# One-core transformer kernel: the first shift and scale made as columns by TensorE, S5's matrices scaled later, the experts' routing weights and masks reordered

## The reference, cut to what matters

```python
c_act = silu(c)
mod = c_act @ w_ada + b_ada                       # [1024] @ [1024, 6144]
sh1, sc1, gt1, sh2, sc2, gt2 = split(mod, 6)
a_in = rmsnorm(h, norm1_g) * (1 + sc1) + sh1
mix = concat(s5_mixer(...), gdn_mixer(...)) @ w_out   # both from a_in @ w_in
h = h + gt1 * mix
m_in = rmsnorm(h, norm2_g) * (1 + sc2) + sh2
moe = hier_moe(m_in, ...)   # 4 groups of 8 experts; per token one group and its top 2 experts
h = h + gt2 * moe
```

## Time and profile before

| | |
|---|---|
| median of 3 runs | 2877.12 us (2876.14 to 2879.36) |
| the profiled execution | 2873.54 us, its span 2871.7 us |
| mean granted clock of TensorE | 0.98 |
| busy: TensorE, its weight load, VectorE, ScalarE, GpSimd | 2752.7, 2308.8, 1597.9, 1233.0, 140.9 us |
| moved by DMA | 509.35 MB, mean 177 GB/s |

### The profile page before, as it was taken

One profiled execution on the slowest core, in us unless ns is written; L12 is line 12 of the kernel. 1 busy time (PEld: TensorE's weight loads), 2 busy tenths in 40 slices (PEclk: granted clock), 3 DMA queues, 4 the chain that ended last, 5 costly groups with the idle time before them and its releaser, 6 DMA issues. The chain is left out here.

```text
span 2871.7 us, 35302 instructions
## 1 busy us (share of the span) xinstructions
PE 2752.7 (96%) x14506; PEld 2308.8 (80%) x14506; DVE 1597.9 (56%) x1821; ACT 1233.0 (43%) x1588; POOL 140.9 (5%) x227
## 2 busy tenths in 40 slices
PE   7988979999999999999998999999999999999998
PEld 6977877888788887888887888888878888896887
DVE  5884467767644536445455645545454464544544
ACT  3202245656534445344344434434453443444443
POOL 4000000000000100001000000000000010010000
PEclk9998989999999999999999999999999999999999
DMA  7432056878655544656553755554435556452652
GB/s 249 156 108 88 30 200 229 310 279 297 220 181 176 167 138 136 207 189 213 193 166 107 240 182 176 191 187 153 144 118 183 195 178 206 155 169 90 225 176 88
DMA packets 349485, 509.35 MB, mean 177 GB/s; under 512 B 14880, under 2 KB 295488, under 8 KB 349328
## 3 DMA queue, kind: packets, MB, share of 16 engines
q1 hardware_dynamic: 342960, 484.17, 49.9%
q0 software_dynamic: 5792, 20.78, 2.1%
q10 hardware_dynamic: 576, 2.20, 0.2%
HBM read 506.04 MB, written 1.05 MB: 177 GB/s over the span
## 5 line engine op out<-in xcount | busy, mean ns | idle before, releaser
L393 DVE TENSOR_TENSOR raw_r<-raw,whi 128x2048 fp32r<-128x2048 f32 x185 | 421.9, 2290 | 170.3 <-ACT whi L385 169.3
L833 ACT ACTIVATE h_hi<-psum 128x256 fp32r<-128x256 f32 x216 | 82.8, 383 | 758.5 <-PE psum L772 684.2
L385 ACT ACTIVATE whi<-raw 128x2048 fp32r<-128x2048 f32 x185 | 351.1, 1909 | 12.4 <-DMA raw<-in_w_up 6.7
L888 DVE TENSOR_TENSOR h_lo<-psum,h_hi 128x256 fp32r<-128x256 f32 x216 | 91.5, 424 | 437.1 <-ACT h_hi L833 437.1
L407 PE MATMUL psum<-place_lo,act_hi 128*128 128x512 f32 (+1 forms) x840 | 318.6, 379 | 0.0
L406 PE MATMUL psum<-whi,act_hi 128*128 128x512 f32 (+1 forms) x872 | 308.2, 353 | 5.4 <-DVE act_lo L639 4.3
L408 PE MATMUL psum<-whi,act_lo 128*128 128x512 f32 (+1 forms) x872 | 302.1, 346 | 0.0
L393 DVE TENSOR_TENSOR place_lo<-arena,place_hi 128x2048 fp32r<-128x2048 f32 x107 | 244.2, 2289 | 91.8 <-ACT place_hi L385 91.8
L407 PE MATMUL psum<-raw_r,act_hi 128*128 128x512 f32 (+1 forms) x808 | 283.8, 351 | 0.0
L406 PE MATMUL psum<-place_hi,act_hi 128*128 128x512 f32 (+1 forms) x592 | 234.1, 395 | 0.0
L408 PE MATMUL psum<-place_hi,act_lo 128*128 128x512 f32 (+1 forms) x592 | 228.6, 386 | 0.0
(11 more groups left out here) (537 smaller groups left out, 5832.7 us busy)
## 6 DMA issues: line engine op xcount, KB each, us to landing
arena<-in_ff_w_in SPq DMA_DIRECT2D x182, 512.0 KB, 4.9
raw<-in_ff_w_in SPq DMA_DIRECT2D x126, 512.0 KB, 4.9
arena<-in_ff_w_out SPq DMA_DIRECT2D x88, 512.0 KB, 4.5
raw<-in_ff_w_out SPq DMA_DIRECT2D x68, 512.0 KB, 4.5
wlo_f<-in_ff_w_in SPq DMA_DIRECT2D x44, 512.0 KB, 4.9
raw<-in_w_ada SPq DMA_DIRECT2D x20, 1024.0 KB, 5.2
raw<-in_w_gate SPq DMA_DIRECT2D x35, 512.0 KB, 4.4
raw<-in_w_up SPq DMA_DIRECT2D x35, 512.0 KB, 5.4
```

What stands on the lines that cost most here:

```text
L385: act.activation(hi, loaded, ACT.Copy).then_inc(S("slab_hi"), 1)
L393: dve.tensor_tensor(lo, loaded, hi.bitcast(F32), ALU.subtract).then_inc(S("slab_lo"), 1)
L833: act.activation(pair_of(turned_h[0], g), gate_up(g)[:, 0:256], ACT.Copy).then_inc(S("pass_turned_hi"), 1)
L888: dve.tensor_tensor(pair_of(turned_h[1], g), gate_up(g)[:, 0:256], pair_of(turned_h[0], g).bitcast(F32), ALU.subtract)\
```

## The change

1. The eight slabs of sh1 and sc1: the slab's 128x128 blocks become the stationary operand and one column of c_act moves past, 16 matmuls per slab instead of 8. The result is a column, 128 values on 128 partitions, in banks 2 and 3. `mod_dve` reads it from there with b_ada (L1157). VectorE's work on `diag` is gone for these slabs, and with it TensorE's wait for it.
2. `s5_c_dve` moves from the start into the projection's loop, behind the split in round 1; the two table parts come directly behind S5's parameters, and x is normalized as soon as slab 4, which lies where the normalized rows go, has been used.
3. In the experts: TensorE makes the slots' routing weights between the halves of pass 0, ahead of the gather; VectorE makes the routing weights around the modulation of the first block, ahead of that block's subtraction and of the first slab splits; ScalarE takes the second exponential and the loading of Silu's table ahead of the first block. The masks are transposed in pass 4 instead of pass 3, and ScalarE copies them there.

```diff
-        def ada_bank(j):
-            return psum[:, 4 + j % 2 if j < ADA_FIRST else 6, 0:256]
+        ada_cols, ada_bank = psum[:, 2:4, 0:KD], psum[:, 6, 0:256]
...
-            if 2 <= j < ADA_FIRST:
-                pe.wait_ge(S("proj_evac"), j - 1)
-            elif j > ADA_FIRST:
+            slab = ada_tiles[b].rearrange("p (k n) -> p k n", k=KD)
+            if j > ADA_FIRST:
                 pe.wait_ge(S("ada_evac"), j - ADA_FIRST)
-            slab = ada_tiles[b].rearrange("p (k n) -> p k n", k=KD)
-            for k in range(KD):
-                last = pe.matmul(ada_bank(j), c_act[:, k:k + 1].to_broadcast([P, P]), slab[:, k, :], start=k == 0, stop=k == KD - 1)
+            for m in range(2 if j < ADA_FIRST else 0):
+                for k in range(KD):
+                    last = pe.matmul(ada_cols[:, j // 4, 2 * (j % 4) + m:2 * (j % 4) + m + 1], slab[:, k, m * P:(m + 1) * P], c_act[:, k:k + 1],
+                                     start=k == 0, stop=k == KD - 1)
+            for k in range(KD if j >= ADA_FIRST else 0):
+                last = pe.matmul(ada_bank, c_act[:, k:k + 1].to_broadcast([P, P]), slab[:, k, :], start=k == 0, stop=k == KD - 1)
...
             for q in (shift, shift + 1):
-                done(dve.tensor_tensor(modc[:, q, :], modc[:, q, :], col("b_ada", q * KD, KD), ALU.add))
+                if q < 2:
+                    dve.wait_ge(S("ada_used"), 4 * q + 4)
+                    ins = dve.tensor_tensor(modc[:, q, :], ada_cols[:, q, :], col("b_ada", q * KD, KD), ALU.add)
...
                 next_lo(dve, "w_in", j, 10)
+                if j == 1:
+                    s5_c_dve(dve, done)
...
                     turn_h_pe(pe, n - 1)
+                if n == 0:
+                    slot_weights_pe(pe)
                 if n < 3:
                     gather_pe(pe, n + 2)
-                elif n == 3:
+                elif n == 4:
                     turn_masks_pe(pe)
                 gate_up_pe(pe, n, 1)
                 if n:
                     down_pe(pe, n - 1)
-                else:
-                    slot_weights_pe(pe)
...
             act.activation(gexp, gexp, ACT.Exp).then_inc(S("group_exp"), 1)
+            act.wait_ge(S("pair_diff"), 1)
+            act.activation(pair_e, pair_e, ACT.Exp).then_inc(S("pair_exp"), 1)
+            act.activation(warm, warm, ACT.Silu)
             block_hi_act(act, 0)
             slab_hi(act, "moe", 0)
             slab_hi(act, "moe", 1)
-            act.wait_ge(S("pair_diff"), 1)
-            act.activation(pair_e, pair_e, ACT.Exp).then_inc(S("pair_exp"), 1)
-            act.activation(warm, warm, ACT.Silu)
...
-                if n == 3:
+                if n == 4:
                     act.wait_ge(S("moe_turned_raw"), 1)
...
-            block_dve(dve, 0)
-            slab_lo(dve, "moe", 0)
-            slab_lo(dve, "moe", 1)
...
             dve.tensor_tensor(pair_e, m2, m1, ALU.subtract).then_inc(S("pair_diff"), 1)
+            block_dve(dve, 0, 0)
             dve.wait_ge(S("group_exp"), 1)
             done(dve.reduce_sum(gden, by(gexp, 4), AX))
             done(dve.reciprocal(gden, gden))
+            block_dve(dve, 0, 1)
             dve.wait_ge(S("pair_exp"), 1)
...
             dve.tensor_tensor(oh1, oh1, oh2, ALU.add).then_inc(S("moe_weights"), 1)
+            block_lo_dve(dve, 0)
+            slab_lo(dve, "moe", 0)
+            slab_lo(dve, "moe", 1)
             dve.wait_ge(S("moe_slot_raw"), 1)
...
-            for j in range(ADA_FIRST):
-                ada_dve(dve, done, j)
-                if j == 0:
-                    s5_c_dve(dve, done)
-                elif j in (2, 4):
-                    s5_table_dve(dve, done, TABLE_SHARED + j // 2 - 1)
+            for lv in (TABLE_SHARED, TABLE_SHARED + 1):
+                s5_table_dve(dve, done, lv)
+            dve.wait_ge(S("ada_used"), 5)
             pre_rows_dve(dve, 0)
             mod_dve(dve, done, 0, "norm1")
```

More of the change, by code:

```diff
@@ L91 @@
 S5_ACT = {"c_act": (1,), "s5_step": (2,), "s5_rad": (3,), "s5_turn": (4, 5)}
-S5_DVE = {"half": (1,), "s5_lr": (2,), "s5_angle": (3,), "turn_pow": (4, 5, 6, 7, 8, 9, 10), "s5_c": (11,), "table_im": (12, 13),
+S5_DVE = {"half": (1,), "s5_lr": (2,), "s5_angle": (3,), "turn_pow": (4, 5, 6, 7, 8, 9, 10), "table_im": (11, 12), "s5_c": (13,),
           "s5_last": (14, 15, 16, 17)}
@@ L1136, in ada_dve @@
             dve.wait_ge(S("ada_used"), j + 1)
-            sem = S("proj_evac" if j < ADA_FIRST else "ada_evac")
             part, c = divmod(j, D // 256)
@@ L1141, in ada_dve @@
                 row = mod[:, j * 256:(j + 1) * 256]
-                dve.tensor_tensor(row, row, ada_bank(j), ALU.add).then_inc(sem, 1)
+                dve.tensor_tensor(row, row, ada_bank, ALU.add).then_inc(S("ada_evac"), 1)
             else:
-                if part < 2:
-                    dve.tensor_tensor(diag[:], ada_bank(j).rearrange("p (k n) -> p k n", k=2), rep(ident, 2), ALU.mult).then_inc(sem, 1)
-                else:
[L1148 to L1156, removed]
+                r = slice(32 * c, 32 * c + 32)
+                picked = diag[r].rearrange("p t n -> p (t n)").rearrange("p (k i) -> p k i", k=KD)
+                dve.tensor_tensor(picked, ada_bank[r].rearrange("p (i k) -> p k i", k=KD),
+                                  ident[r, r].unsqueeze(1).to_broadcast([32, KD, 32]), ALU.mult).then_inc(S("ada_evac"), 1)
+                dve.wait_ge(S("ada_evac"), j - ADA_FIRST + 1)
+                done(dve.reduce_sum(modc[r, part - 1, :], picked, AX))
         def mod_dve(dve, done, shift, norm):
             for q in (shift, shift + 1):
-                done(dve.tensor_tensor(modc[:, q, :], modc[:, q, :], col("b_ada", q * KD, KD), ALU.add))
+                if q < 2:
+                    dve.wait_ge(S("ada_used"), 4 * q + 4)
+                    ins = dve.tensor_tensor(modc[:, q, :], ada_cols[:, q, :], col("b_ada", q * KD, KD), ALU.add)
+                    ins.then_inc(S("proj_evac"), 4)
+                    dve.wait_ge(S("proj_evac"), 4 * q + 4)
+                else:
+                    done(dve.tensor_tensor(modc[:, q, :], modc[:, q, :], col("b_ada", q * KD, KD), ALU.add))
             dve.scalar_tensor_tensor(modc[:, shift + 1, :], modc[:, shift + 1, :], 1.0, col(norm, 0, KD), ALU.add, ALU.mult)\
@@ L1988, in moe_act, with block_dve, block_lo_dve @@
             slab_hi(act, "ff0a", FF_HEAD[1])
-        def block_dve(dve, q):
-            b = BLOCK_ORDER[q]
[L1992 to L1998, removed]
+        def block_dve(dve, q, half):
+            dve.wait_ge(S("moe_gathered"), 2 * q + half + 1)
+            for c in range(4):
+                k = 4 * half + c
+                last = dve.tensor_scalar(mod_part(q, half)[:, c * P:(c + 1) * P], gathered(q, half)[:, c * P:(c + 1) * P],
+                                         modc[:, 3, k:k + 1], modc[:, 2, k:k + 1], ALU.mult, ALU.add)
+            last.then_inc(S("moe_block_f"), 1)
+        def block_lo_dve(dve, q):
+            b = BLOCK_ORDER[q]
             for half in range(2):
@@ L2099, in moe_dve @@
                 if n < 4:
-                    block_dve(dve, n + 1)
+                    block_dve(dve, n + 1, 0)
+                    block_dve(dve, n + 1, 1)
+                    block_lo_dve(dve, n + 1)
                 moe_h_dve(dve, n)
```

## The result

| | before | after |
|---|---|---|
| median of 20 runs each, us | 2879.06 (2874.62 to 2884.87) | 2881.24 (2878.32 to 2889.15) |
| ratio after / before, 95% interval | | 1.0014 (1.0007 to 1.002) |
| profiled span, us | 2871.7 | 2877.8 |
| TensorE busy, us (records) | 2752.7 (14506) | 2774.1 (14634) |

The forecast was 2881.4 us with a range of 2872 to 2889. The interval of the ratio is 2.0 to 5.8 us slower, around the forecast's +4.3. The change is three moves that nearly cancel, so the total proves little; the places do.

What follows compares the result with a forecast made beforehand. TensorE, busy for 96% of the span, was taken to bound the kernel. Terms of 17.4 - 6.3 - 6.8 = +4.3 us, added to the median 2877.12, gave 2881.4 us, range 2872 to 2889.

Steps and rivals of the forecast that it cites:

- The start, +17.4: Eight slabs as one-column matmuls: TensorE stays at 1.2 GHz, 6.8 us a slab, so ScalarE starts at 65.1, not 47.70.
- The Trainium skill's sentence: "Activity releases the throttle": if any matmul counts, the slab stage's clock rises, giving 2858 us; the prediction doubted that reading.
- S5's matrices, 0: VectorE's six scaling operations moved into the projection: TensorE late by 0 to 2.1 us, taken as 0.
- the lower bound: Lower price of VectorE's six moved scaling operations in the projection: 0.6 us each, done at 76.5; upper 1.10 each.
- Routing weights, -6.3: Weights made between pass 0's halves: its h is turned at 406.8 instead of 413.14, -6.3 us.
- rival B: Experts' first passes: late transfer or clock fall in pass 0, only 6 to 9 us won, 2885 to 2889 us; 20%.
- Masks a pass later, -6.8: Masks turned in pass 4: pass 3's down product starts at about 451.9, not 458.75, -6.8 us.
- The sum: Whole kernel: 17.4 - 6.3 - 6.8 = +4.3 us, forecast 2881.4 us against the median 2877.12.
- Rival A: Clock rises in the new slab stage: slabs take 3.6 us, sum -19, 2858 us; chance 6%.
- C (split late): Projection: the split behind S5's matrices is late, 1.5 to 2.1 us more, 2883 us; chance 8%.
- D (cheaper start): Slabs as columns cost only 8 to 13 us, clock rising partway or projection starting at 2.4 GHz: 2872 to 2877 us; 8%.

Runs made afterwards that it cites:

- part 1 alone: Kernel before with only the eight slabs made columns, S5's matrices still scaled at the start, experts as before: 2895.74 us against 2878.0, ratio 1.0061.
- fillers: Changed kernel with 36 matmuls of 128 columns, results unused, behind the fourth slab of one-column matmuls: 2893.04 us in one run.
- part 3 alone: Kernel before with only the experts' routing weights and masks moved as in the change, start as before: 2866.40 us, ratio 0.9963.
- the masks alone: Kernel before with one edit, masks turned in pass 4 instead of pass 3: 2872.64 us, ratio 0.998.
- weights-alone: Kernel before with the routing weights made in pass 0, masks still turned in pass 3: 2872.68 us, ratio 0.9981.

## Why the prediction was right, point by point

- **The start, +17.4: right.** +17.7 us by time with part 1 alone, 18.0 in its trace. The steps hold one by one: 6.83 us a slab for 6.8 taken, the end of the last slab at 64.7 for 63.9 (0.6 of it is the later first slab), ScalarE at 65.88 for 65.1, the first projection matmul at 72.13 for 71.4. The reason, that the narrow matmuls stay at 1.2 GHz, is shown by the run with 128 columns (more work on the same weights in half the time) and by the one-column slab that took 3.50 us behind fillers.
- **The Trainium skill's sentence** that activity releases the throttle ("TensorE: Matmul & The Clock Gate", Part 1), read so that any matmul counts, would have given 2858 us. The runs do not agree with that reading: the array was in use without a gap for 55 us and stayed at half pace.
- **S5's matrices, 0: right**, and the lower bound too: 0.69 us each, not 1.10. What I had not said is that they would have brought the projection forward by 2.3 us had part 1 not covered them.
- **Routing weights, -6.3: the mechanism right, the size off in the changed kernel's trace.** 6.4 us with part 3 alone; in the changed kernel 4.8. The term that failed is "pass 0 starts as before and its half 0 ends" 2.89 us later. The clock fell in half 0, 1.25 us, and was still down in the weights, 0.3 us. This is the part of rival B that speaks of the clock, though not by its reason: the narrow weights came after the fall. And the fall is not the change's: half 0 ran slow as well with part 1 alone and with the masks alone, where the weights stand in their old place. Compared like with like the gain is the same. With the fall in both, 22.25 us from the start of pass 0 to the turning of its h (part 1 alone) become 15.88; with it in neither, 20.71 become 14.32: 6.4 us each time. The before of the forecast was simply an execution without the fall. Rival B's other part, a late transfer that ends the chain, did not come: ScalarE waited 1.80 us for a slab in pass 0, but nothing of TensorE's ended on it.
- **Masks a pass later, -6.8: right** in three traces, 14.07 us for the stretch in the changed kernel and with the masks alone, and ended by the copies of the masks in ScalarE as worked out. The terms listed for ScalarE in the forecast add up to 8.2 to 8.5 us, not to the 7.9 that it took from them; the trace has 7.9 (455.77 to 463.70), since each operation starts some 0.1 us before the row of the one ahead of it ends.
- **The sum.** Measured in the trace, the terms are +18.2, 0, -4.8 and -6.8; together +6.6 where the span has +6.1. In between, 1.6 of the 18.2 is given back up to pass 0, nearly all of it by differences of the clock. At the start of the projection 0.9 us: the clock had come up at 69.0 us, behind the transposes, and the projection was slow only from some 72.5 to 75.9 us (the windows above), where before it was slow from its first matmul to some 59.5. By 131 us of the old trace 0.75 of that is lost again, where a stretch at half clock lasts 13.7 us and not 10.2. And 1.7 us come at 200 us, where the old trace runs from 199.8 to 203.2 at half clock and the new one, at 217, does not. The wait ahead of pass 0 takes 0.3 back (3.54 us for 3.21). Whether the change has a part in these differences the runs do not show. Behind the experts 1.1 us is lost in small steps, spread from 485 to 1809 us. The forecast of +4.3 is 1.8 us under the span's difference, mostly by the clock in pass 0. By the medians of the runs the change costs 2.2 us, by the ratio's interval 2.0 to 5.8; 4.3 lies inside that and 6.1 just outside. That the time itself, 2881.24, lies 0.2 us from the forecast is luck: the forecast was added to a median of 3 runs, 2877.12, and with 20 runs the kernel before stands at 2879.06.
- **Rival A (the clock rises)** did not come about with one column, but its time is real: 128 columns bring it. **C (split late)** and **D (cheaper start)** did not show.

What is left open of the clock in pass 0: of the eleven traces without fillers there, half 0 ran at full clock in four (waits ahead of it of 3.21 to 3.30 us) and slow in seven (3.43 to 3.83 us). The two sides hold one and the same kernel, 128 columns; here is its second run:

```profile
383.78 0.47 PE L406 MATMUL psum<-whi,blocks_r 128*128 128x512 f32 x1 [3.43 <-DVE raw_r L393]
...
386.53 0.63 PE L406 MATMUL psum<-whi,blocks_r 128*128 128x512 f32 x1
```

In the first run the wait was 3.26 and half 0 ran at 0.40 us a matmul; h was turned 14.34 us behind the start of pass 0, here 15.90. So it differs from execution to execution of one kernel, and no part of the change makes it by itself. That the wait alone decides is not shown: in the weights-alone trace the clock fell after a wait of 3.22 us too, only later, and in before it fell at 404.3 us, in a wait of 2.62. Open also is what makes the wait differ; I didn't try to steer it.

## What to carry to other kernels

A matmul that is made narrower may save nothing: here its time was the loading of its weights (3.63 us a slab with 1 column, 3.73 with 128, both at full clock), and the clock that the wide ones brought up did not come. Look for the same kind of narrow matmul elsewhere in the trace, and at which clock it ran: that gave 6.8 us a slab before anything was built. Widening the moving operand with a stride of zero (the same column read again and again) cost 0.1 us a slab, and it took some 22 us off the changed kernel (-19.5 us against the kernel before, where that had +2.2). And take a change with terms of both signs apart: here each half of part 3 was worth having, and part 1 hid it. When a stage is compared between two single traces, look first whether the clock was the same in both; here that alone moved a term by 1.5 us.

## What the runs showed that was not expected

- 64 moving columns did nothing for the clock (20.72 us for the first 96 records; 20.61 with one column), with 128 it came up (13.07 us). I had left open which it would be.
- In the run with fillers in the middle one-column matmuls ran at the raised clock from 47.52 to some 52 us, then it fell with TensorE never idle.
- The clock column of the profile reads 1.00 until its first record, even where the pace is half for 55 us.
- The same kind of operation of VectorE on 512 elements takes 0.69 us in the projection and 1.10 at the start, where GpSimd works beside it. That GpSimd slows VectorE is not isolated. The reverse a run shows: GpSimd's operation L1246 on 256 elements took 1.07 us in before (at 18.89, beside L1273 and L1274); in the run with the slabs as before, where S5's matrices are gone from there, the same operation (L1247 there) took 0.62 (at 19.24).
